# Folding the modulation row behind the first piece of the next unit, and three more units' sums on VectorE

## The chip, the cores and the metric

The kernel runs on one core of a Trainium2 chip. The time is the device time of one execution in microseconds (us), from three runs of the same program. Lower is better.

## The reference, cut to what matters

Two models run one behind the other on the same 256 tokens of width 2048. The first has two layers (`first_block`): a norm, one wide projection `w_in` to 5824 columns, three kinds of attention, a gate and the projection `w_out`. The second has one layer of another kind with a mixture of experts behind it, and its norms are modulated by a row `mod` that depends on nothing but the vector `c`:

```python
def second_block(x, c, ..., ada_w, ada_b, ...):
    c_act = jax.nn.silu(c)                              # 1 x 2048
    mod = (c_act @ ada_w[l] + ada_b[l])[:, None, :]     # 2048 x 12288, a product with one row
    sh1, sc1, g1, sh2, sc2, g2 = jnp.split(mod, 6, axis=-1)
    ...
```

The kernel computes this row while the layers of the first model run, 512 of its 12288 columns at a time, so in 24 parts: 12 in each layer of the first model.

## The kernel before, in words

**Units and pieces.** In each of the two layers (`l` is 0 or 1) TensorE goes through 16 units. Units 0 to 11 are the column blocks of `w_in`, 512 columns each, in the order `ORDER`; unit 2 (`NARROW`) is the narrow one of 192 columns. Units 12 to 15 are `w_out`. A unit is cut into 8 pieces (4 in unit 2) of two 128-row blocks of weights. ScalarE rounds a piece's weights (`w_hi`, L2489), GpSimd computes what the rounding left (L2172), and TensorE multiplies: `by_hi` is eight products with the rounded weights (L2248), `by_lo` four with the remainder (L2259). In `unit` the `by_lo` of a piece comes behind the `by_hi` of the next one. The rounded pieces stand in a ring of four buffers, so ScalarE can be up to four pieces ahead of the last piece that TensorE has finished.

**Steps between the pieces.** Attention for the columns that are already there is cut into steps (transposes, scores, weighted sums), and `unit` is given a list of (piece, step). Before piece `i` it takes the steps placed at `i` or earlier. The order on every engine is written out by hand, and engines run in order: what stands behind a wait waits too.

**The modulation's parts.** Part `p` of layer `l` needs two half loads of `ada_w` (2 MB each), which use ring slots 2 and 3, one behind the other, in the queue of SyncE (`Halves`, L2110). A slot is free when `ada_used` says that the half before it was used up. There are two ways to compute a part. By TensorE: `ada(l, p)` behind the last piece of unit `p` multiplies the 16 blocks of `ada_w` by a column of `c` each (L2298), into four rows of the bank `psTD`; VectorE then adds up the four rows and the bias (`add_row`, L2932 to L2935). By VectorE, for the parts named in `BY_VECTOR`: `mods` does 16 multiply-adds over 128x512 (L2909, L2911), which leave the products summed over the 16 blocks in `ada_sum`, and TensorE only sums over the partitions with one product (L2303), still in `ada` behind the last piece of unit `p`; `add_row` then has one instruction (L2938).

**What stands around part 2 and part 3.** Behind unit 2 come `mla_norm` (transposes) and `mla_up` (products, L2361), and then `ada(l, 2)`. On VectorE the loop turn `p = 2` is: `add_row(2)`, which waits for TensorE's sum; `rotations` (two calls of `rotate`, twelve `TENSOR_TENSOR`, L2775 to L2777); then `mods` of part 3, if it is VectorE's; then the tasks of unit 3, of which there are none. On ScalarE, `store_row(2)` (L2602, and L2597 in `load_b`) waits for the row of `add_row(2)`, and behind it in the same queue come the roundings from piece 3 of unit 3 on. At the top of the turn `p = 3` comes `add_row(3)`.

Of the kernel before, what the change touches and what calls it, by code (L numbers as in the profile page):

```python
# [90 lines left out]
         9: (2, 3, 4, 5, 5, 6, 7), 10: (1, 2, 2, 3, 4, 5, 6, 7, 7, 8), 11: (1, 2, 2, 3, 4, 5, 5, 6, 6, 7, 7, 8),  # L91
         12: (1, 2, 3, 4, 4, 5, 5, 6, 6, 7, 7, 8, 8), 13: (2,)}
MODS = 16
BY_VECTOR = ((0, 2, 4, 5, 6), (2, 4, 5, 6))
MOD_AT = {4: {("mla_rope", 0, 0): 4, ("mla_rope", 0, 1): 9, "end": 16}, 5: {("soft", "M0", 0): 2, ("soft", "M0", 1): 5, ("soft", "M1", 0): 9, "end": 16},
          6: {("out", "M0", 0): 3, ("out", "M0", 1): 8, ("prep_d", 0, 0): 14, "end": 16}}
X_AT = {0: (14, 1), 1: (14, 5), 2: (15, 4), 3: (0, 4)}
# [1777 lines left out]
def program(nc, ctx, a, out):  # L1875
# [4 lines left out]
    def sb(name, shape, dt=f32):  # L1880
        return ctx.enter_context(nc.sbuf_tensor(name, shape, dt))

    def sem(name):
        return ctx.enter_context(nc.semaphore(name))

    def both(name, shape):
# [21 lines left out]
    ada_sum = cb[:, :, :].rearrange("p k n -> p (k n)")  # L1908
# [14 lines left out]
    half = sb("minus_half", [P, 8])  # L1923
# [9 lines left out]
    psS, psO, psTA, psTD = bank[4], bank[5], bank[6], bank[7]  # L1933
# [6 lines left out]
    hu_used, pc_used, ada_used = sem("half_unit_used"), sem("piece_used"), sem("ada_half_used")  # L1940
    x_in, spilled = [sem(f"x_in{n}") for n in range(4)], [sem(f"x_spilled{n}") for n in range(4)]
    x_back, x_hi_ready, sqx_ready, mla_in, in_cst, row_summed = (
        sem(n) for n in ("x_back", "x_rounded", "x_squares", "mla_weights_in", "cst_in", "ada_row_summed"))
# [4 lines left out]
    ta_ready, ta_copied, td_ready, td_copied = (sem(n) for n in ("ta_ready", "ta_copied", "td_ready", "td_copied"))  # L1948
# [120 lines left out]
    def rounded(q):  # L2069

        _, _, _, _, _, ks, width = piece(q)
        return w_hi[:, q % HI_RING, 0:len(ks) * width]
# [16 lines left out]
    def sums(p):  # L2089

        return p + (4 if p > NARROW else 0)
# [109 lines left out]
    def _(pe):  # L2201
# [3 lines left out]
        ta, td = Tally(0, 1), Tally(0, 1)  # L2205
# [5 lines left out]
        def transposes(by_act, sources):  # L2211

            t, ready, cop, ps = (ta, ta_ready, ta_copied, psTA) if by_act else (td, td_ready, td_copied, psTD)
            pe.wait_ge(cop, t.now())
            for i, src in enumerate(sources):
                last = nc.tensor.transpose(ps[:, i * P:(i + 1) * P], src, ident)
            last.then_inc(ready, 1)
            t.next()
# [6 lines left out]
        def x_chunk(l, n):  # L2225

            pe.wait_ge(xo, 1 + 4 * (l - 1) + n + 1) if l else pe.wait_ge(x_in[n], 16)
            for j in (2 * n, 2 * n + 1):
                transposes(j % 2 == 0, [X[:, t, (2 * j + b) * P:(2 * j + b + 1) * P] for b in (0, 1) for t in range(TT)])
                x_done[l, j] = (ta if j % 2 == 0 else td).now()  # L2230
# [5 lines left out]
        def by_hi(q, v, first):  # L2236

            l, u, i, key, _, ks, width = piece(q)
            hi, lo = (x_hi, x_lo) if u < 12 else (y_hi, y_lo)
            if u == 0 or u >= 12:  # L2240
                j = ks[0] // 2
                pe.wait_ge(td_copied if j % 2 else ta_copied, (x_done if u == 0 else y_done)[l, j])
            pe.wait_ge(w_hi_ready, q + 1)
            w = rounded(q).rearrange("p (k n) -> p k n", n=width)
            for part in (hi, lo):
                for n, k in enumerate(ks):
                    for t in range(TT):
                        nc.tensor.matmul(bank[2 * (v % 2) + t][:, 0:width], part(k, t), w[:, n, :],  # L2248
                                         start=first and part is hi and n == 0, stop=False)

        def by_lo(q, v, end):

            l, u, i, key, _, ks, width = piece(q)
            hi = x_hi if u < 12 else y_hi
            pe.wait_ge(w_lo_ready, q + 1)
            w = weights(q, True).rearrange("p (k n) -> p k n", n=width)
            for n, k in enumerate(ks):
                for t in range(TT):
                    last = nc.tensor.matmul(bank[2 * (v % 2) + t][:, 0:width], hi(k, t), w[:, n, :],  # L2259
                                            start=False, stop=end and n == len(ks) - 1)  # L2260
            last.then_inc(pc_used, 1)

        def unit(l, u, steps, bank_free):

            base, n = l * NPC + FIRST[u], PIECES_IN[u]
            queue, behind = list(steps), None
            for i in range(n):
                while queue and queue[0][0] <= i:
                    queue.pop(0)[1]()
                if u < 12:  # L2270
                    v, first, end = sums(u), i == 0, i == n - 1
                    if i == 0:
                        bank_free()
                else:
                    col, rows = OUT_HALVES[2 * (u - 12) + i // 4]
                    v, first, end = 16 + col, rows == 1 and i % 4 == 0, rows == 0 and i % 4 == 3
                    if first:
                        bank_free(col)
                by_hi(base + i, v, first)
                if behind:  # L2280
                    by_lo(*behind)
                behind = (base + i, v, end)
            by_lo(*behind)
            for _, do in queue:
                do()

        def ada(l, p):

            if l + p == 0:
                pe.wait_ge(half_ready, 1)  # L2290
            pe.wait_ge(td_copied, td.now())
            if p not in BY_VECTOR[l]:
                for j in (0, 1):
                    pe.wait_ge(w_in[2 + j], HALVES.loaded["a", l, p, j])
                    w = ring[:, 2 + j, :].rearrange("p (k n) -> p k n", k=8)
                    for k in range(8):
                        g = k % 4
                        last = nc.tensor.matmul(psTD[32 * g:32 * g + 1, :], ccol[:, 8 * j + k:8 * j + k + 1], w[:, k, :],  # L2298
                                                start=j == 0 and k < 4, stop=j == 1 and k >= 4)
                    last.then_inc(ada_used, 1)  # L2300
            else:
                pe.wait_ge(ada_used, 24 * l + 2 * p + 2)
                nc.tensor.matmul(psTD[0:1, :], half[:, 0:1], ada_sum, start=True, stop=True).then_inc(row_summed, 1)  # L2303
            td.next()

        def qk_columns(by_act, group, sources):
# [41 lines left out]
        def mla_norm(l):  # L2348

            pe.wait_ge(cn_ready, l + 1)  # L2350
            cq = lambda b, t: PROJ[:, t, CQ + b * P:CQ + (b + 1) * P]
            for bs in ((0, 1), (2, 3), (4,)):
                transposes(False, [cq(b, t) for b in bs for t in range(TT)])
# [78 lines left out]
        for l in range(LAYERS):  # L2432
            for u in range(12):

                def bank_free():
                    v = sums(u)
                    if v >= 2:
                        pe.wait_ge(pj_copied, 16 * l + v - 1)
                    elif l:
                        pe.wait_ge(xo, 1 + 4 * (l - 1) + 3 + v)  # L2440

                later = steps(l, u)
                if u == 0:
                    later += [((X_AT[3][1] if l else 0), lambda n=n: x_chunk(l, n)) for n in range(4) if n == 3 or not l]
                unit(l, u, later, bank_free)
                if u == NARROW:
                    mla_norm(l)
                    mla_up(l)
                ada(l, u)

            def out_free(col):
                pe.wait_ge(pj_copied, 16 * l + 15 + col) if col < 2 else pe.wait_ge(xo, 1 + 4 * l + col - 1)

            for u in range(12, UNITS):
                later = steps(l, u)
                for n in range(3) if l < LAYERS - 1 else ():
                    if X_AT[n][0] == u:
                        later.append((X_AT[n][1], lambda n=n: x_chunk(l + 1, n)))
                unit(l, u, later, out_free)
# [232 lines left out]
    def _(dve):  # L2692
# [231 lines left out]
        def add_row(l, p):  # L2924
# [3 lines left out]
            if n > 0:  # L2928
                dve.wait_ge(mod_out, 16 * n)
            if p not in BY_VECTOR[l]:  # L2930
                dve.wait_ge(ada_used, 2 * n + 2)
# [4 lines left out]
            else:  # L2936
                dve.wait_ge(row_summed, l * len(BY_VECTOR[0]) + sum(x < p for x in BY_VECTOR[l]) + 1)
                V.scalar_tensor_tensor(ada_row[:, :], psTD[0:1, :], -2.0, ada_b[:, :], ALU.mult, ALU.add).then_inc(td_copied, 1)  # L2938
# [31 lines left out]
        for l in range(LAYERS):  # L2970
# [34 lines left out]
            for p, u in enumerate(ORDER):  # L3005
# [5 lines left out]
                if early:  # L3011
                    task(l, p + 1, *early[0])
                if p and p in BY_VECTOR[l]:
                    mods(l, p, MODS)
# [5 lines left out]
                if p == NARROW:  # L3020
                    rotations(l)
                if p + 1 in BY_VECTOR[l]:
                    mods(l, p + 1, mod_at.table.get("begin", 0) if p + 1 in MOD_AT else MODS)
# [95 lines left out]
```

## Time and profile before

| what | value |
|---|---|
| median of 3 runs | 2451.64 us (2450.39 to 2454.13) |
| the profiled execution | 2450.62 us, span of its trace 2448.8 us |
| TensorE busy | 94% of the span |
| VectorE, ScalarE, GpSimd busy | 37%, 35%, 37% |
| mean granted TensorE clock | 0.983 of full speed |
| first model (both layers) | about 0 to 945 us of the span |

The times of the trace count from the start of the span. A row of a timeline gives the start, the length, the engine, the line of the kernel and the operation, what it writes and reads, how many instructions the row holds, and in brackets how long the engine stood idle before it and what ended that. A granted clock of 1.00 is TensorE's upper level, 2.4 GHz, and 0.50 the lower, 1.2 GHz.

### The profile page before, as it was taken

The page shows a single profiled execution, that of the slowest core. Times are in us where ns is not written, and L with a number is a line of the kernel's source. Part 1 is how long each engine was busy: PE and PEld are TensorE (multiplying, and loading weights), DVE is VectorE, ACT ScalarE, POOL GpSimd, SP SyncE. Part 2 cuts the span into 40 slices and gives each one's busy share as a digit, 9 for nine tenths or more (in the row PEclk, how much of TensorE's full clock was granted, in tenths as well). Part 3 has the DMA queues.
Part 4 walks back from the last instruction along what each step waited for, and adds up shares of the span by engine and source line. Part 5 has one row for each costly group of instructions (what it writes and reads, how often), then busy time and mean ns, then how long its engine had stood idle before and what let it go on. Part 6 is the DMA issues. An engine that isn't in the chain of part 4 may idle for free.

```text
span 2448.8 us, 29997 instructions
## 1 busy us (share of the span) xinstructions
PE 2304.2 (94%) x11863; PEld 1522.7 (62%) x11863; DVE 912.7 (37%) x1495; ACT 852.4 (35%) x1583; POOL 899.5 (37%) x395
## 2 busy tenths in 40 slices
PE   7999999999999998999899898999999999999997
PEld 5677777876777787778787685444444444444442
DVE  5555543125555346155443742122222222222223
ACT  5344454533444443543324742122212221212111
POOL 5566656866666587874333471000000000000000
PEclk9999999999999999999999998999999999999999
DMA  8677665686776661532222329999999999999996
GB/s 325 265 295 287 274 244 238 223 322 251 275 288 253 265 249 62 188 138 87 88 102 99 145 89 393 422 427 428 428 429 428 428 428 428 428 429 428 428 428 269
DMA packets 60805, 716.54 MB, mean 293 GB/s; under 512 B 11024, under 2 KB 11632, under 8 KB 17184
## 3 DMA queue, kind: packets, MB, share of 16 engines
q1 hardware_dynamic: 58800, 712.25, 71.2%
q10 hardware_dynamic: 1904, 2.86, 0.3%
q8 instruction: 73, 1.20, 0.2%
q14 instruction: 28, 0.23, 0.0%
HBM read 710.85 MB, written 4.24 MB: 292 GB/s over the span
## 4 chain that ended last, share of the span: by engine, by line
issue 39%; PE 16%; DVE 3%; ACT 2%; DMA 1%; DVEq 0%; POOLq 0%; POOL 0%; ACTq 0%
PE bank L380 5%; PE bank L434 2%; PE bank L390 2%; PE bank L444 1%; DMA weight_ring<-in_w_in_dram 1%; PE bank L519 1%; PE bank L525 1%; ACT w_hi_parts L2489 1%; PE bank L523 1%; PE bank L623 1%; PE bank L482 0%; PE bank L483 0%; PE bank L480 0%; PE bank L473 0%; PE bank L366 0%
## 5 line engine op out<-in xcount | busy, mean ns | idle before, releaser
L2172 POOL TENSOR_TENSOR weight_ring_parts<-weight_ring,w_hi_parts 128x1024 fp32r<-128x1024 f32 (+2 forms) x368 | 871.9, 2390 | 554.8 <-ACT w_hi_parts L2489 553.3
L2489 ACT ACTIVATE w_hi_parts<-weight_ring 128x1024 fp32r<-128x1024 f32 (+2 forms) x368 | 376.7, 1042 | 435.9 <-PE bank L2259 175.5
L1509 POOL TENSOR_TENSOR rms_out<-rms_in,minus_half 128x2 f32<-128x2 f32 x2 | 1.4, 698 | 963.6 <-DVE rms_in L1855 950.4
L1592 PE MATMUL bank<-weight_ring,qk_t 128*64 128x512 f32 x1024 | 229.2, 603 | 17.8 <-DMA weight_ring<-in_expert_w_up_dram 17.8
L2248 PE MATMUL bank<-w_hi_parts,h_t_parts 128*128 128x512 f32 (+1 forms) x768 | 213.3, 401 | 2.0 <-ACT w_hi_parts L2489 2.0
L2248 PE MATMUL bank<-w_hi_parts,x_res_parts 128*128 128x512 f32 (+1 forms) x768 | 198.5, 382 | 0.0
L2259 PE MATMUL bank<-weight_ring_parts,h_t_parts 128*128 128x512 f32 (+1 forms) x768 | 193.3, 380 | 0.0
L1592 PEld LDWEIGHTS bank<-weight_ring,qk_t 128*64 128x64 f32 x1024 | 77.4, 139 | 166.6 <-issue 166.6
L2248 PEld LDWEIGHTS bank<-w_hi_parts,h_t_parts 128*128 128x128 f32 x768 | 133.0, 190 | 47.1 <-issue 17.4
L2248 PEld LDWEIGHTS bank<-w_hi_parts,x_res_parts 128*128 128x128 f32 x768 | 140.5, 189 | 29.6
L2259 PEld LDWEIGHTS bank<-weight_ring_parts,h_t_parts 128*128 128x128 f32 x768 | 139.8, 188 | 28.4
L1833 DVE TENSOR_TENSOR dist<-dist_masked,bank 128x512 f32<-128x512 f32 x16 | 11.0, 688 | 351.0 <-PE bank L1592 351.0
L1818 DVE SCALAR_TENSOR_TENSOR qk_t<-bank,slot_gate,proj 128x512 f32<-128x512 f32 x64 | 48.1, 751 | 240.9 <-PE bank L1623 240.9
L1689 ACT ACTIVATE p_t<-bank 128x512 f32<-128x512 f32 x16 | 9.6, 597 | 344.3 <-PE bank L1605 344.3
L1541 PE MATMUL bank<-p_buf,y 128*128 128x128 f32 x1024 | 123.3, 280 | 4.2 <-ACT qk_t L1668 3.1
L1592 PE MATMUL bank<-w_hi,qk_t 128*64 128x512 f32 x256 | 114.3, 600 | 12.0 <-DMA h_t<-in_expert_w_up_dram 12.0
L1541 PEld LDWEIGHTS bank<-p_buf,y 128*128 128x128 f32 x1024 | 119.0, 195 | 7.1 <-ACT qk_t L1668 5.9
L1592 PE MATMUL bank<-h_t,qk_t 128*64 128x512 f32 x256 | 114.5, 601 | 0.0
L1623 PE MATMUL bank<-weight_ring,p_t 128*64 128x512 f32 x512 | 113.0, 594 | 0.8 <-ACT p_t L1689 0.8
L1592 PE MATMUL bank<-proj,qk_t 128*64 128x512 f32 x512 | 112.8, 593 | 0.0
L380 PE MATMUL bank<-w_hi_parts,h_t_parts 128*128 128x512 f32 (+1 forms) x352 | 97.8, 400 | 7.3 <-ACT w_hi_parts L2489 5.7
L1668 ACT ACTIVATE qk_t<-bank,conv_w_t 128x128 f32<-128x128 f32 x256 | 94.5, 456 | 19.5 <-PE bank L1541 19.5
(473 smaller groups left out, 3581.1 us busy)
## 6 DMA issues: line engine op xcount, KB each, us to landing
weight_ring<-in_w_in_dram SPq DMA_DIRECT2D x64, 2048.0 KB, 7.6
weight_ring<-in_ada_w_dram SPq DMA_DIRECT2D x48, 2048.0 KB, 12.5
weight_ring<-in_expert_w_gate_dram SPq DMA_DIRECT2D x32, 2048.0 KB, 26.9
weight_ring<-in_expert_w_up_dram SPq DMA_DIRECT2D x32, 2048.0 KB, 18.3
weight_ring<-in_expert_w_down_dram SPq DMA_DIRECT2D x32, 2048.0 KB, 24.1
weight_ring<-in_w_out_dram SPq DMA_DIRECT2D x24, 2048.0 KB, 8.7
proj<-in_expert_w_gate_dram SPq DMA_DIRECT2D x16, 2048.0 KB, 26.8
proj<-in_expert_w_up_dram SPq DMA_DIRECT2D x16, 2048.0 KB, 15.4
```

What stands on the lines that cost most here:

```text
L380: mm(bank[2 * (v % 2) + t][:, 0:width], part[:, k, t * P:(t + 1) * P], w[:, n, :], start=first and part is hi and n == 0, stop=False)
L390: last = mm(bank[2 * (v % 2) + t][:, 0:width], hi[:, k, t * P:(t + 1) * P], w[:, n, :], start=False, stop=end and n == len(ks) - 1)
L434: mm(bank[2 * (p % 2) + t][:, :], y_at(part, kb, t), w[:, n, :], start=r == FIRST2[c] and part == "hi" and n == 0, stop=False)
L1541: last = mm(ps[:, i * P:(i + 1) * P], H[:, t, k * P:(k + 1) * P], m.gm[:, t, :], start=t == 0, stop=t == TT - 1)
L1592: last = mm(bank[side][s, :], m.xg[:, 8 * j + k, s], weights(hu + e, 8)[:, k, :], start=j == 0 and k == 0, stop=j == 1 and k == 7)
L1623: last = mm(bank[4 + n % 2][s, :], m.hidt[:, f, s], weights(hu + e, 4)[:, f, c * U:(c + 1) * U], start=f == 0, stop=f == 3)
L1668: last = A_(m.xg[:, k, :], bank[2 + (tx.n - 1) % 2][:, i * P:(i + 1) * P], ACT.Identity, scale=m.gsc2[:, k:k + 1], bias=m.shc2[:, k:k + 1])
L1818: V.scalar_tensor_tensor(m.ye[:, c], bank[4 + n % 2][:, :], m.slot_gate[:, :], m.g2[:, c], ALU.mult, ALU.mult).then_inc(m.dn_copied, 1)
L2172: nc.gpsimd.tensor_tensor(weights(split, True), weights(split, False), rounded(split).bitcast(f32), ALU.subtract)\
L2248: nc.tensor.matmul(bank[2 * (v % 2) + t][:, 0:width], part(k, t), w[:, n, :], start=first and part is hi and n == 0, stop=False)
L2259: last = nc.tensor.matmul(bank[2 * (v % 2) + t][:, 0:width], hi(k, t), w[:, n, :], start=False, stop=end and n == len(ks) - 1)
L2489: A_(rounded(split), weights(split, False), ACT.Copy).then_inc(w_hi_ready, 1)
```

## The change

Parts 1 and 3 of layer 1 and part 3 of layer 0 move from TensorE to VectorE (`BY_VECTOR`). For the parts 0 to 5 that are VectorE's, the product that sums over the partitions moves from the end of unit `p` to the place before piece 1 of unit `p + 1`, so behind `by_hi` of piece 0 (`FOLD_AT`, `fold`); it stands ahead of other steps with the same place. Part 6 stays behind its unit. Nothing else is changed: `mods` and `add_row` keep their places in VectorE's order.

```diff
-BY_VECTOR = ((0, 2, 4, 5, 6), (2, 4, 5, 6))
+BY_VECTOR = ((0, 2, 3, 4, 5, 6), (1, 2, 3, 4, 5, 6))
+FOLD_AT = {0: 1, 1: 1, 2: 1, 3: 1, 4: 1, 5: 1}
...
-            pe.wait_ge(td_copied, td.now())
             if p not in BY_VECTOR[l]:
+                pe.wait_ge(td_copied, td.now())
...
                     last.then_inc(ada_used, 1)
-            else:
-                pe.wait_ge(ada_used, 24 * l + 2 * p + 2)
-                nc.tensor.matmul(psTD[0:1, :], half[:, 0:1], ada_sum, start=True, stop=True).then_inc(row_summed, 1)
+                td.next()
+            elif p not in FOLD_AT:
+                fold(l, p)
+
+        def fold(l, p):
+
+            pe.wait_ge(td_copied, td.now())
+            pe.wait_ge(ada_used, 24 * l + 2 * p + 2)
+            nc.tensor.matmul(psTD[0:1, :], half[:, 0:1], ada_sum, start=True, stop=True).then_inc(row_summed, 1)
             td.next()
...
+                if u - 1 in BY_VECTOR[l] and u - 1 in FOLD_AT:
+                    later = sorted([(FOLD_AT[u - 1], lambda: fold(l, u - 1))] + later, key=lambda x: x[0])
                 unit(l, u, later, bank_free)
```

## Rows read from the trace of the kernel before

**Rows 1.** The page's first part: busy time of each engine, share, instructions.

```profile
PE 2304.2 (94%) x11863; PEld 1522.7 (62%) x11863; DVE 912.7 (37%) x1495; ACT 852.4 (35%) x1583; POOL 899.5 (37%) x395
```

**Rows 2.** Timeline of TensorE, layer 0, from the end of `mla_up` into unit 4.

```profile
107.37 1.02 PE L2303 MATMUL bank<-ada_sums,minus_half 128*1 128x512 f32 x2
108.32 1.19 PE L2248 MATMUL bank<-w_hi_parts,h_t_parts 128*128 128x512 f32 x4
...
130.31 3.62 PE L2298 MATMUL bank<-weight_ring,c_col 128*1 128x512 f32 x32
133.85 1.20 PE L2248 MATMUL bank<-w_hi_parts,h_t_parts 128*128 128x512 f32 x4
...
135.80 0.60 PE L2216 MATMUL bank<-cst,proj 128*128 128x128 f32 x4
```

**Rows 3.** Timeline of VectorE, layer 0: sums of part 2, its row, the rotations.

```profile
90.81 0.75 DVE L2909 TENSOR_SCALAR bank<-weight_ring,c_col 128x512 f32<-128x512 f32 x1
...
102.67 0.75 DVE L2911 SCALAR_TENSOR_TENSOR ada_sums<-weight_ring,c_col,bank 128x512 f32<-128x512 f32 x1
108.53 0.68 DVE L2938 SCALAR_TENSOR_TENSOR ada_part<-bank,ada_part 1x512 f32<-1x512 f32 x1 [5.12 <-PE bank L2303]
109.37 0.42 DVE L2775 TENSOR_TENSOR rope_q<-proj,cos_t 128x256 f32<-128x256 f32 x1 [0.16 <-DVE ada_part L2938]
...
111.88 2.38 DVE L2775 TENSOR_TENSOR rope_k<-proj,cos_t 128x128 f32<-128x128 f32 x1
...
119.71 0.29 DVE L2777 TENSOR_TENSOR rope_k<-rope_k,rope_tmp 128x128 f32<-128x128 f32 x1
```

**Rows 4.** Timeline of ScalarE, its queue and GpSimd in the same stretch of layer 0.

```profile
109.30 0.23 ACTq L2602 DMA_DIRECT2D mod_scratch<-ada_part  x1
...
110.52 1.06 ACT L2489 ACTIVATE w_hi_parts<-weight_ring 128x1024 fp32r<-128x1024 f32 x1 [1.95 <-issue]
...
111.66 2.45 POOL L2172 TENSOR_TENSOR weight_ring_parts<-weight_ring,w_hi_parts 128x1024 fp32r<-128x1024 f32 x1 [10.83 <-ACT w_hi_parts L2489]
...
113.25 1.06 ACT L2489 ACTIVATE w_hi_parts<-weight_ring 128x1024 fp32r<-128x1024 f32 x1 [1.67 <-PE bank L2259]
...
114.39 2.40 POOL L2172 TENSOR_TENSOR weight_ring_parts<-weight_ring,w_hi_parts 128x1024 fp32r<-128x1024 f32 x1 [0.28 <-ACT w_hi_parts L2489]
...
121.35 1.06 ACT L2489 ACTIVATE w_hi_parts<-weight_ring 128x1024 fp32r<-128x1024 f32 x1 [1.66 <-PE bank L2259]
```

**Rows 5.** Timeline of VectorE and GpSimd in layer 0 from 277 us.

```profile
277.73 9.83 POOL L2172 TENSOR_TENSOR weight_ring_parts<-weight_ring,w_hi_parts 128x1024 fp32r<-128x1024 f32 x4
...
278.64 1.52 DVE L2850 SCALAR_TENSOR_TENSOR row_rec<-row_rec,lam,row_sum 128x2 f32<-128x2 f32 x1
...
280.20 5.11 DVE L2852 SCALAR_TENSOR_TENSOR p_buf<-p_buf,row_rec 128x256 f32<-128x256 f32 x2
```

**Rows 6.** TensorE after an idle stretch, and windows (busy times, then clock, DMA).

```profile
951.03 4.53 PE L366 MATMUL bank<-p_t,proj 128*128 128x128 f32 x24 [6.08 <-DVE p_t L1047]
...
951.03:956.03 5.00, 4.66 (x25) 4.49 (x26) 1.99 (x4) 0.76 (x2) 4.92 (x3) 0.66 0.00 0
1095.68:1101.68 6.00, 6.00 (x31) 6.00 (x32) 1.32 (x2) 0.42 (x1) 4.22 (x2) 0.54 0.01 3
```

**Rows 7.** Timelines of layer 1: TensorE around units 3 and 4, and VectorE's last rotation.

```profile
567.45 1.02 PE L2303 MATMUL bank<-ada_sums,minus_half 128*1 128x512 f32 x2
...
590.40 3.61 PE L2298 MATMUL bank<-weight_ring,c_col 128*1 128x512 f32 x32
...
595.89 0.60 PE L2216 MATMUL bank<-cst,proj 128*128 128x128 f32 x4
...
579.80 0.29 DVE L2777 TENSOR_TENSOR rope_k<-rope_k,rope_tmp 128x128 f32<-128x128 f32 x1
```

**Rows 8.** Loads of `ada_w`: issues of two halves, a wait for one, layer 1's unit 1.

```profile
132.27 2.04 SPq L2110 DMA_DIRECT2D weight_ring<-in_ada_w_dram  x2
...
142.84 0.75 DVE L2909 TENSOR_SCALAR bank<-weight_ring,c_col 128x512 f32<-128x512 f32 x1 [2.52 <-DMA weight_ring<-in_ada_w_dram]
...
508.81 2.04 SPq L2110 DMA_DIRECT2D weight_ring<-in_ada_w_dram  x2
...
532.37 3.61 PE L2298 MATMUL bank<-weight_ring,c_col 128*1 128x512 f32 x32
```

## The prediction, made before the changed kernel was run

> **What bounds the kernel now.** I read the page's busy shares first, then the timeline of TensorE around each `ada`, then those of the engines that feed it. TensorE is busy for 94% of the span, the others for some 37% [rows 1]. In the two layers its timeline has almost no bracket: from one unit into the next it goes without a stop, so whatever is taken off its list is gained, if nothing new comes late. A part by TensorE holds it from 130.31 to 133.85, 3.54 us; a part by VectorE only from 107.37 to 108.32, 0.95 us [rows 2]. So the question is not what the 32 removed instructions cost, but whether VectorE has the sum ready when TensorE gets to it. For that the reader has to look at what VectorE does ahead of the sums: in turn 2 it waits for TensorE's product (5.12 us in the bracket), then rotates from 109.37 to 120.00, and would begin the sums of part 3 only then [rows 3].
>
> **Part 1 of layer 1.** It takes away 3.54 and adds 0.95: 2.6 us gained, if the sum is ready. The halves are issued from 508.81 on; elsewhere VectorE got the first half 10.6 us after the issue (132.27 to 142.84) [rows 8], so here at 519.4. The sixteen sums of part 2 took from 90.81 to 103.42, 12.6 us [rows 3]; here they end at about 532.0. TensorE ends unit 1 at 532.37 [rows 8] and asks behind piece 0, about 2 us later. Ready, by some 2 us. The slots come free earlier than before, so the loads behind it are not later. VectorE's row sum is one instruction rather than four, and the norm behind it waits for ScalarE's squares, as it does now. Gain 2.6 us.
>
> **Moving the product of part 2, layer 0.** The product leaves the front of unit 3 and comes behind piece 0's eight products, which take 1.95 us (133.85 to 135.80) [rows 2]. TensorE's own list is as long as before. But everything that waits for the product is 1.95 us later: `add_row(2)` begins at 110.48, the rotations at 111.3. ScalarE is caught as well: `store_row(2)` waits for that row, and the rounding of piece 3 stands behind it (110.52, right behind the store at 109.30), and GpSimd's remainder for it starts at 111.66 [rows 4]. Now that becomes 113.6. Before, GpSimd was kept to TensorE's pace from there: the next rounding waited for TensorE (113.25) and left a gap of 0.28 us on GpSimd [rows 4]. TensorE's own pace for pieces 1 and on is unchanged, so the roundings of pieces 4 to 7 keep nearly their times (the last begins at 121.35 [rows 4]), while GpSimd is 2 us behind. Its five instructions then run back to back, from 113.6 on.
>
> This matters to the rotations, which read two operands from SBUF each. In the trace such an instruction takes 0.42 us undisturbed, and 2.38 us where GpSimd is at work (111.88) [rows 3]. Where GpSimd has gaps, a second rotation slips through between two of its instructions; three of the twelve are held up and the end is 120.00. Where it has none, each such instruction of VectorE costs a whole one of GpSimd: against four GpSimd instructions in 9.83 us, one took 1.52 and the next two 5.11 together [rows 5]. So the rotations 7 to 11 cost 2.46 us each (9.83 / 4): five GpSimd instructions from 113.6 end at 125.9, the last rotation at 126.2. That is 6.2 us later than now: 1.95 by the place, 4.25 by the loss of the gaps.
>
> The Trainium skill (SBUF — State Buffer, "Who interferes with whom") says that an instruction of VectorE with two SBUF inputs and one of GpSimd that reads SBUF lock each other out for a whole instruction, and that "Issue order, not op shape, decides who blocks". The rows agree on the size, and it is the rule that speaks against this change. Taken literally, VectorE might get in first and hold up GpSimd, by a few tenths each time; the rotations would then end at about 122 and the time would be that of the first rival below. The sums of `mods` read one operand from SBUF and one from a bank, which by the same section is free of the lock.
>
> **Part 3, layer 0.** The sums start at 126.2, take 12.6 us, and end at 138.8. They can't start earlier: they stand behind the rotations in VectorE's order, and all their data has long been there. TensorE, without the product ahead of unit 3 and with it inside, ends the unit at 130.31 as before, does piece 0 of unit 4 until 132.26, and waits there, with the whole rest of unit 4 behind the wait. The product starts at 138.9 and ends at 139.85. At this same point of its list it is at 135.80 now [rows 2]. So this part, which was to give 2.6 us, costs 4.05, and TensorE stands idle for 6.65 us.
>
> **The clock after such a stop.** After 6.08 us of idle time TensorE had a granted clock of 0.66 over the next 5 us, so 3.4 us of it at the lower level (1.2 GHz), a loss of 1.7 us. After another stop it had 0.54 over 6 us, a loss of 2.8 us [rows 6]. I take 1.7, the stop that is nearest in length; the bounds are 0 and 2.8.
>
> **Parts 2 and 3, layer 1.** The same chain, 2.6 us earlier on TensorE. Unit 3 starts at 567.45 - 2.6 = 564.85, the product at 566.8, so 0.65 us before its present time. The rotations end at 580.1 now [rows 7]; I take 580.1 - 0.65 + 4.25 = 583.7, the sums end at 596.3, the product at 597.35, against 595.89 for the same point now [rows 7]: 1.45 us lost with the 2.6 us of part 1 already counted. The clock takes another 1.7.
>
> **Parts 0, 4 and 5** are moved only. Their products are 0.95 us wherever they stand, and VectorE gets 1.95 us more for them; their rows come 1.95 us later, ahead of tasks that wait for steps at piece 1 or 2 of the unit anyway. In unit 4 the sums of part 4 wait for their load until 142.84 [rows 8], about as long as the new stop lasts. Nothing, between -0.5 and +0.5 us in all.
>
> **The sum.** Layer 0: 4.05 + 1.7 = +5.75. Layer 1: 1.45 + 1.7 = +3.15. Together +8.9 on the profiled execution's 2450.62: 2459.5. The median of the runs is 1.02 above that execution, so I forecast 2460.5 us.
>
> **The rivals.**
>
> *The rotations keep their length.* VectorE's instructions find gaps, or get in first. Then only the 1.95 us count: the sums of part 3 end at 134.6 in layer 0, and TensorE passes the point at 135.65 for 135.80 now; in layer 1 at 593.1 for 595.89. That is -0.2 and -2.8, with stops of 2.3 us, and between 0 and 1.7 us of clock each: -3.0 to +0.4, a median of 2448.7 to 2452.1, say 2450.4. For it: two of the twelve slipped through a gap in the trace of before. Against it: they did so only where GpSimd had a gap.
>
> *The sums are hidden, and the change does what it says on paper* (the rival on the other side, faster). Three parts give 2.6 us each, 7.8 in all: 2443.8. The mechanism is that the sums of part 3 overlap with the rotations' place or end by 132.26; it decides at 2.4 us less on VectorE than even the first rival needs. Nothing in the rows offers that.
>
> *More stops than these.* If the loads of part 1 in layer 1 land over 2.3 us later than the row that I used says, the product waits in unit 2 too and the norm behind it slides, 1 to 4 us; or each stop costs 2.8 us of clock and a sixth rotation is held up: up to 8.9 + 2 x 1.1 + 2 x 2.5 = +16, 2468.
>
> *That the change doesn't do what it says* can be left out: the moved product and the three parts are in the lists of all engines.
>
> **How the numbers follow.** The forecast (rotations held up for the whole of GpSimd's stretch, one or two of them more or less, clock 0 to 2.8) 0.60; rotations as now 0.26; hidden 0.05; more stops 0.09. The forecast's own range is +5.5 (no clock) less one slipped rotation in a layer (2.5), to +11.1: 2454.6 to 2462.7. For 8 in 10 the range takes in most of the first rival above and the beginning of the last: 2451 to 2465. A measurement of this kernel can tell about 0.2%, 4.9 us, from no change. Over 2456.5 lies most of the forecast and all of the last rival: 0.62. Within lies the rest of the forecast and nearly all of the first rival: 0.33. Faster by over 0.2%: 0.05.
>
> **What would show each step.** In the trace after: a bracket of 6 to 7 us ahead of L2303's product in unit 4 of both layers, released by VectorE's sums; seven or eight of the twelve rotations undisturbed and five at about 2.5 us, with GpSimd's five instructions without a gap between them; a clock below 1.00 in the 5 us behind each bracket; no bracket at the product in unit 2 of layer 1, and TensorE 2.6 us earlier there against layer 0's delay. Brackets of 2 us would mean the first rival, none the second. The forecast is wrong if GpSimd's gaps stay, because then the largest term, 4.25 us in each layer, is gone.

## The result, and the profile after

The changed kernel takes 2459.09 us (median of 7 runs, 2457.05 to 2465.87), against 2451.64 for the kernel before, measured beside it (median of 7 runs, 2447.38 to 2454.13). The ratio is 1.004, with a 95% interval of 1.0027 to 1.0052; it is estimated from all runs of both kernels and isn't the quotient of the two medians, which is 1.003. The changed kernel is slower by 0.4%. The forecast was 2460.5, in a range of 2451 to 2465. The profiled execution of the changed kernel took 2459.09 us with a span of 2457.3 us.

The page's busy shares hardly moved, as in [rows 1]; what changed is when the engines work:

```profile
PE 2301.7 (94%) x11773; PEld 1522.5 (62%) x11773; DVE 952.9 (39%) x1534; ACT 851.8 (35%) x1583; POOL 897.8 (37%) x395
```

TensorE's timeline in layer 0, units 2 to 4, to be read against [rows 2] (columns: start, duration, engine, line, operation; the bracket is idle time before the row and what ended it):

```profile
106.73 1.50 PE L2249 MATMUL bank<-w_hi_parts,h_t_parts 128*128 128x512 f32 x4
...
109.08 1.02 PE L2310 MATMUL bank<-ada_sums,minus_half 128*1 128x512 f32 x2
...
130.20 1.16 PE L2249 MATMUL bank<-w_hi_parts,h_t_parts 128*128 128x512 f32 x4
...
138.47 1.87 PE L2310 MATMUL bank<-ada_sums,minus_half 128*1 128x512 f32 x2 [6.21 <-DVE ada_sums L2920]
140.27 1.11 PE L2217 MATMUL bank<-cst,proj 128*128 128x128 f32 x4
```

Unit 3 begins at 106.73 without its product, which now comes behind piece 0, at 109.08. Unit 3 ends, and unit 4 begins, at 130.20; before, unit 3 ended at 130.31 and part 3's 32 products came next. Then the bracket that was not there before: TensorE stands for 6.21 us and is released by VectorE's last sum of part 3. The transposes that follow are at 140.27, where they were at 135.80 [rows 2].

VectorE, ScalarE and GpSimd in the same stretch, against [rows 3, 4]:

```profile
110.24 0.68 DVE L2947 SCALAR_TENSOR_TENSOR ada_part<-bank,ada_part 1x512 f32<-1x512 f32 x1 [6.95 <-PE bank L2310]
111.07 0.43 DVE L2784 TENSOR_TENSOR rope_q<-proj,cos_t 128x256 f32<-128x256 f32 x1 [0.16 <-DVE ada_part L2947]
...
111.58 1.06 ACT L2498 ACTIVATE w_hi_parts<-weight_ring 128x1024 fp32r<-128x1024 f32 x1 [3.16 <-DVEq L2949]
...
112.72 12.40 POOL L2173 TENSOR_TENSOR weight_ring_parts<-weight_ring,w_hi_parts 128x1024 fp32r<-128x1024 f32 x5 [11.64 <-ACT w_hi_parts L2498]
...
113.12 2.51 DVE L2786 TENSOR_TENSOR rope_q<-rope_q,rope_tmp 128x256 f32<-128x256 f32 x1
115.67 2.37 DVE L2784 TENSOR_TENSOR rope_k<-proj,cos_t 128x128 f32<-128x128 f32 x1
117.96 2.49 DVE L2785 TENSOR_TENSOR rope_tmp<-proj,sin_t 128x128 f32<-128x128 f32 x1
120.48 2.38 DVE L2786 TENSOR_TENSOR rope_k<-rope_k,rope_tmp 128x128 f32<-128x128 f32 x1
122.89 2.37 DVE L2784 TENSOR_TENSOR rope_k<-proj,sin_t 128x128 f32<-128x128 f32 x1
125.19 0.28 DVE L2785 TENSOR_TENSOR rope_tmp<-proj,cos_t 128x128 f32<-128x128 f32 x1
...
126.49 11.05 DVE L2920 SCALAR_TENSOR_TENSOR bank<-weight_ring,c_col,bank 128x512 f32<-128x512 f32 x14
137.58 0.75 DVE L2920 SCALAR_TENSOR_TENSOR ada_sums<-weight_ring,c_col,bank 128x512 f32<-128x512 f32 x1
```

The row of part 2 is added at 110.24 (before: 108.53), and ScalarE's rounding of piece 3, which waits for it, starts at 111.58 (before: 110.52). GpSimd's five remainders are one group of 12.40 us with no gap, and exactly five rotations take 2.4 to 2.5 us each, one for each of GpSimd's instructions. The rotations last from 111.07 to 125.79, 14.7 us, for 10.6 before (109.37 to 120.00). The sums behind them end at 138.3.

Layer 1, TensorE, against [rows 7]:

```profile
551.26 0.66 PE L2217 MATMUL bank<-cst,proj 128*128 128x128 f32 x4 [0.97 <-DVE qk_t L2749]
...
553.95 7.98 PE L2368 MATMUL bank<-y,qk_t 128*128 128x512 f32 x24 [0.62 <-issue]
...
593.06 1.16 PE L2249 MATMUL bank<-w_hi_parts,h_t_parts 128*128 128x512 f32 x4 [1.31 <-ACT w_hi_parts L2498]
...
600.03 1.87 PE L2310 MATMUL bank<-ada_sums,minus_half 128*1 128x512 f32 x2 [4.89 <-DVE ada_sums L2920]
601.83 1.12 PE L2217 MATMUL bank<-cst,proj 128*128 128x128 f32 x4
...
607.04 0.60 PE L2217 MATMUL bank<-cst,proj 128*128 128x128 f32 x4
```

The same stop, 4.89 us, and one of 1.31 us ahead of it that was in no step of the prediction: TensorE waits for the rounded weights of unit 4. The first row serves to follow part 1: the same transposes start at 548.29 in the kernel before.

**Where the time went.** I compare the two traces at points that both have. From the end of unit 0 of layer 0 (49.44 before, 49.18 after) to the end of unit 0 of layer 1 (506.85, 512.43) it is 457.41 and 463.25: **+5.84 us for layer 0**. From there to the wait that ends the first model, [rows 6] at 951.03 and in the changed kernel

```profile
957.38 2.93 PE L367 MATMUL bank<-p_t,proj 128*128 128x128 f32 x12 [6.07 <-DVE p_t L1048]
```

it is 444.18 and 444.95: **+0.77 us for layer 1**. I call this point the end of the first model. The code behind it is the same in both kernels and took 1497.8 and 1499.9 us in these two executions. In the ten profiled executions of this study it took between 1497.8 and 1501.9, so single executions scatter there by more than most terms of the sum, and below I set the times of this point beside the medians.

### The profile page after: what moved, and what is told of

It reads as the page before. It is cut to its first block, busy times and chain, and to the rows that moved or that the text cites. A ratio compares the mean times of both kernels' runs of the same rounds, so it can differ in the third digit from the quotient of the medians.

```text
span 2457.3 us, 29863 instructions
## 1 busy us (share of the span) xinstructions
PE 2301.7 (94%) x11773; PEld 1522.5 (62%) x11773; DVE 952.9 (39%) x1534; ACT 851.8 (35%) x1583; POOL 897.8 (37%) x395
## 4 chain that ended last, share of the span: by engine, by line
issue 39%; PE 17%; DVE 3%; ACT 2%; DMA 1%; DVEq 0%; POOLq 0%; POOL 0%; ACTq 0%
PE bank L381 5%; PE bank L391 2%; PE bank L435 2%; PE bank L445 1%; PE bank L520 1%; DMA weight_ring<-in_w_in_dram 1%; PE bank L526 1%; PE bank L524 1%; ACT w_hi_parts L2498 1%; PE bank L624 1%; PE bank L483 0%; PE bank L484 0%; PE bank L481 0%; PE bank L474 0%; PE bank L367 0%
## 5 line engine op out<-in xcount | busy, mean ns | idle before, releaser
L2920 DVE SCALAR_TENSOR_TENSOR bank<-weight_ring,c_col,bank 128x512 f32<-128x512 f32 x168 | 126.8, 755 | 5.4
```

The source lines that it names most:

```text
L2920: ins = V.scalar_tensor_tensor(acc if k < MODS - 1 else ada_sum, w, ccol[:, k:k + 1], acc, ALU.mult, ALU.add)
```

## The experiments

All eight are the changed kernel with one thing altered, and each was timed in rounds with the kernel before. The ratio is to that kernel, with its 95% interval; the last column is the start of the product that marks the end of the first model in the profiled execution. The ratio isn't the quotient of a row's median and the 2451.64: the runs of the kernel before that each experiment was timed beside had medians of 2452.98 (sums alone, part 2's product back, sums first, rounding ahead) and 2452.21 (the other four).

| kernel | median us | ratio (95%) | end of first model |
|---|---|---|---|
| before | 2451.64 | | 951.03 |
| after | 2459.09 | 1.0040 (1.0027 to 1.0052) | 957.38 |
| sums alone | 2450.53 | 0.9997 (0.9987 to 1.0006) | 948.88 |
| place alone | 2453.47 | 0.9997 (0.9987 to 1.0008) | 949.98 |
| part 1 alone | 2448.24 | 0.9986 (0.9976 to 0.9996) | 947.92 |
| part 2's product back | 2444.94 | 0.9971 (0.9960 to 0.9982) | 942.37 |
| sums first | 2446.62 | 0.9978 (0.9968 to 0.9987) | 943.14 |
| rounding ahead | 2451.86 | 0.9994 (0.9985 to 1.0003) | 953.30 |
| no remainder | 2443.34 | 0.9964 (0.9949 to 0.9978) | 941.73 |
| part 1 too | 2444.67 | 0.9970 (0.9958 to 0.9981) | 943.01 |

The theory on trial is that of the prediction: the later place of part 2's product takes the gaps from GpSimd, the rotations are then held up for all of its stretch, and the sums of part 3 behind them are late. The rivals are that the sums are late by themselves, that the later place alone is enough, and that VectorE's load as such is the cause.

### The sums alone, with all products in their old places

```diff
-FOLD_AT = {0: 1, 1: 1, 2: 1, 3: 1, 4: 1, 5: 1}
+FOLD_AT = {}
```

> The three parts move to VectorE, and every product over the partitions stays at the end of its unit. My theory (the moved product of part 2 makes the sums of part 3 late: 1.95 us by its place, some 4 us because GpSimd then runs without gaps and holds up the rotations): the rotations end at 120.0 in layer 0 as before the change, the sums of part 3 at 132.6, TensorE asks for them at 130.3, so it stands for 2.4 us at the end of unit 3 in each layer, not for 5 to 6 us; part 1 gives 2.6 us; in all -3.0 us against before, plus 0 to 1.7 us of lower clock for each stop: 2448 to 2452. Rival A (VectorE's list is simply too long for part 3, wherever the product of part 2 stands): the stop is at least as long as with the change, 6 us, since TensorE asks 2 us sooner, and the time is 2459 or more.

Measured: 2450.53 us, as expected, and no difference from before that the interval shows. Its TensorE waits for the sums of part 3 in both layers:

```profile
132.34 1.02 PE L2310 MATMUL bank<-ada_sums,minus_half 128*1 128x512 f32 x2 [2.30 <-DVE ada_sums L2920]
...
590.85 1.36 PE L2310 MATMUL bank<-ada_sums,minus_half 128*1 128x512 f32 x2 [2.30 <-DVE ada_sums L2920]
```

The rotations last from 109.04 to 119.66, 10.6 us as in [rows 3]. For part 3 the move therefore saves 2.6 us and gives back 2.30. In layer 0 the stop of the changed kernel is 2.7 times as long, so the sums by themselves are not its cause.

### Part 2's product back in front of unit 3, all else as in the change

```diff
-FOLD_AT = {0: 1, 1: 1, 2: 1, 3: 1, 4: 1, 5: 1}
+FOLD_AT = {0: 1, 1: 1, 3: 1, 4: 1, 5: 1}
```

> The whole change, but the product of part 2 stays at the end of its unit; those of parts 0, 1, 3, 4 and 5 are moved. My theory: rotations as before the change (three of twelve held up, end at 120.0 in layer 0), sums of part 3 end at 132.6, TensorE asks at 132.3 and stands for 0.5 us; each part gives its 2.6 us less that: -6.8 us against before, 2445, and no stretch at the lower clock in unit 4. Rival A (VectorE's list is too long for part 3 anyway): stops of 5 us or more in unit 4, 2457 or more. Rival B (a moved product costs something by itself, by breaking up the pieces or by keeping ScalarE's stores late): about 2450, with no stop.

Measured: 2444.94 us, as expected, and faster than both kernels. VectorE, GpSimd and TensorE in layer 0, then TensorE in layer 1:

```profile
112.17 2.37 DVE L2784 TENSOR_TENSOR rope_k<-proj,cos_t 128x128 f32<-128x128 f32 x1
114.46 0.28 DVE L2785 TENSOR_TENSOR rope_tmp<-proj,sin_t 128x128 f32<-128x128 f32 x1
114.69 2.40 POOL L2173 TENSOR_TENSOR weight_ring_parts<-weight_ring,w_hi_parts 128x1024 fp32r<-128x1024 f32 x1 [0.30 <-ACT w_hi_parts L2498]
114.77 2.47 DVE L2786 TENSOR_TENSOR rope_k<-rope_k,rope_tmp 128x128 f32<-128x128 f32 x1
117.28 0.29 DVE L2784 TENSOR_TENSOR rope_k<-proj,sin_t 128x128 f32<-128x128 f32 x1
...
132.98 1.02 PE L2310 MATMUL bank<-ada_sums,minus_half 128*1 128x512 f32 x2 [0.32 <-DVE ada_sums L2920]
...
585.41 1.16 PE L2249 MATMUL bank<-w_hi_parts,h_t_parts 128*128 128x512 f32 x4 [0.94 <-ACT w_hi_parts L2498]
...
587.41 1.02 PE L2310 MATMUL bank<-ada_sums,minus_half 128*1 128x512 f32 x2
```

A held-up rotation and a quick one alternate: GpSimd has its gaps again (0.22 to 0.30 us) and the rotations take 10.6 us. The stop of 2.30 is down to 0.32, because part 3's own product still stands behind piece 0 (2.30 - 1.95 = 0.35). In layer 1 there is no stop at the product; the 0.94 us ahead of it is a wait for unit 4's weights, which is taken up below. This one number in a table is worth 957.38 - 942.37 = 15.0 us at the end of the first model. Two stops of 6.21 and 4.89 us, less the 0.32, and the lower clock behind them (1.6 and 2.8, below) make 15.2.

### The new places alone, with the sums of before

```diff
-BY_VECTOR = ((0, 2, 3, 4, 5, 6), (1, 2, 3, 4, 5, 6))
+BY_VECTOR = ((0, 2, 4, 5, 6), (2, 4, 5, 6))
```

> The products of parts 0, 2, 4 and 5 (and of none besides) are moved behind the first piece of the next unit, and parts 1 and 3 stay with TensorE as before the change. My theory: the rotations are held up as with the change and end at about 126 in layer 0, but nothing waits for them before unit 4: TensorE has no stop, the time is that of before, within 1 us; at most a few tenths are gained where VectorE was late by 0.6 us at part 6. Rival B (moving the products costs by itself): 1 to 2 us slower for each moved product, 2455 or more.

Measured: 2453.47 us, as expected no difference from before. VectorE's first and last held-up rotations and GpSimd's group:

```profile
113.66 12.39 POOL L2173 TENSOR_TENSOR weight_ring_parts<-weight_ring,w_hi_parts 128x1024 fp32r<-128x1024 f32 x5 [12.06 <-ACT w_hi_parts L2498]
114.06 2.52 DVE L2786 TENSOR_TENSOR rope_q<-rope_q,rope_tmp 128x256 f32<-128x256 f32 x1
...
123.84 2.37 DVE L2784 TENSOR_TENSOR rope_k<-proj,sin_t 128x128 f32<-128x128 f32 x1
```

The place alone brings GpSimd's closed group and the five held-up rotations, 14.7 us in all, and here it costs nothing, because no sums of part 3 stand behind them. So neither half of the change is slow. The stop needs both.

### The sums of part 3 ahead of the rotations on VectorE

```diff
-                if p == NARROW:
-                    rotations(l)
                 if p + 1 in BY_VECTOR[l]:
                     mods(l, p + 1, mod_at.table.get("begin", 0) if p + 1 in MOD_AT else MODS)
+                if p == NARROW:
+                    rotations(l)
```

> The whole change, and on VectorE the sums of part 3 come ahead of the rotations. My theory: the sums run from 111.3 to 124 in layer 0, free of GpSimd, the rotations behind them end at about 130, TensorE finds the sums ready in unit 4: no stop in either layer, -7.8 us against before, 2444. Rival C (the rotations are then what comes late: they run into GpSimd's next stretch from 130 on at 2.5 us each, and the copies of unit 4 stand behind them): a stop of 2 to 6 us in unit 4 ahead of the transposes, 2446 to 2456.

Measured: 2446.62 us, faster than before, but 2.6 us above the 2444 that I expected. At the end of the first model the 7.8 us are there (951.03 less 943.14 is 7.9); the medians show only some 5.4 of them (a ratio of 0.9978). In the two profiled executions the unchanged code behind that point took 1500.1 us and, in the kernel before, 1497.8, the least of the ten; why the rest is lost stays open. VectorE and GpSimd in layer 0, then TensorE's product of part 3 in layer 0 and in layer 1:

```profile
112.13 11.05 DVE L2920 SCALAR_TENSOR_TENSOR bank<-weight_ring,c_col,bank 128x512 f32<-128x512 f32 x14
112.99 9.49 POOL L2173 TENSOR_TENSOR weight_ring_parts<-weight_ring,w_hi_parts 128x1024 fp32r<-128x1024 f32 x4 [10.65 <-ACT w_hi_parts L2498]
...
123.99 1.33 DVE L2784 TENSOR_TENSOR rope_q<-proj,cos_t 128x256 f32<-128x256 f32 x1
...
128.79 0.29 DVE L2786 TENSOR_TENSOR rope_k<-rope_k,rope_tmp 128x128 f32<-128x128 f32 x1
...
132.32 1.02 PE L2310 MATMUL bank<-ada_sums,minus_half 128*1 128x512 f32 x2
...
587.53 1.02 PE L2310 MATMUL bank<-ada_sums,minus_half 128*1 128x512 f32 x2
```

Both brackets are gone. The sums run beside GpSimd at 0.79 us each (11.05 / 14), as they do without it, and GpSimd keeps 2.37 us per instruction (9.49 / 4). The rotations behind it find GpSimd nearly done and take 5.1 us. VectorE does the same work in both orders, so its load as such is not the cause; the order is. That the sums aren't disturbed agrees with the Trainium skill (SBUF — State Buffer, "Who interferes with whom"), by which a VectorE instruction with at most one SBUF input, outside the modes that use two ports, doesn't contend with GpSimd. Each sum reads one 128x512 operand from SBUF, a column of `c` beside it, and the running sum from a bank.

### ScalarE's rounding ahead of the store of part 2's row

```diff
-                split_to(q + sum_place(p) + AHEAD)
+                split_to(q + sum_place(p) + AHEAD + (1 if p == NARROW else 0))
                 store_row(l, p)
```

> The whole change, and ScalarE rounds piece 3 of unit 3 before it waits for the row of part 2, not behind it, so that GpSimd gets it some 3 us earlier and is kept to TensorE's pace from there, with its gaps. My theory: the gaps let a second rotation through, the rotations end at about 122.4 in layer 0 and not at 125.8, the stop in unit 4 is 3 us and not 6.2, in both layers: 6 to 7 us less than with the change, some 2452 with the lower clock still paid. Rival D (the hold-up has nothing to do with the gaps; each rotation that meets GpSimd waits for a whole instruction): the rotations end within 1 us of 125.8 and the time stays at 2459.

Measured: 2451.86 us, as expected. GpSimd gets the first rounded piece before the row is stored. Its rows in layer 0, and TensorE's stops:

```profile
115.95 2.46 POOL L2173 TENSOR_TENSOR weight_ring_parts<-weight_ring,w_hi_parts 128x1024 fp32r<-128x1024 f32 x1 [2.46 <-ACT w_hi_parts L2498]
118.61 2.53 POOL L2173 TENSOR_TENSOR weight_ring_parts<-weight_ring,w_hi_parts 128x1024 fp32r<-128x1024 f32 x1 [0.20 <-ACT w_hi_parts L2498]
121.33 2.42 POOL L2173 TENSOR_TENSOR weight_ring_parts<-weight_ring,w_hi_parts 128x1024 fp32r<-128x1024 f32 x1 [0.19 <-ACT w_hi_parts L2498]
...
136.58 1.02 PE L2310 MATMUL bank<-ada_sums,minus_half 128*1 128x512 f32 x2 [2.75 <-DVE ada_sums L2920]
...
597.18 1.02 PE L2310 MATMUL bank<-ada_sums,minus_half 128*1 128x512 f32 x2 [2.80 <-DVE ada_sums L2920]
```

With gaps of 0.2 us back between GpSimd's instructions the rotations take 11.2 us (112.73 to 123.91) rather than 14.7. The product of part 2 is as late as in the change, and yet the stop falls from 6.21 to 2.75. That separates the two terms of the prediction: some 3.5 us are the lost gaps. The 2.75 that are left are the 0.32 us that stay even with part 2's product back, the 1.95 of the place and the 0.5 or so by which these rotations are longer than 10.6, together 2.8.

### GpSimd's remainders of unit 3 nearly left out

```diff
-                nc.gpsimd.tensor_tensor(weights(split, True), weights(split, False), ...
+                n = 8 if left_out(split) else weights(split, True).shape[-1]
+                nc.gpsimd.tensor_tensor(weights(split, True)[:, 0:n], weights(split, False)[:, 0:n], ...
```

> The whole change, but for the pieces 3 to 7 of unit 3, in both layers, GpSimd's remainder is computed over 8 columns only, and TensorE takes the rounded weights a second time in its place. That leaves out part of the projection of unit 3, so it measures the hold-up of the rotations alone and is no version of the kernel. My theory (GpSimd's instructions hold them up): all twelve rotations at 0.42 or 0.29 us, done within some 5 us of the row of part 2 in place of 14.9, the sums of part 3 ready at about 128.5 in layer 0, ahead of TensorE, no stop and no lower clock in unit 4 of either layer; first model 14 us shorter than with the change, 2444. Rival E (they are slow for another reason, such as the loads or ScalarE's writes): five of them still take 2.4 us each and the stop stays at 6.

Two things aren't in these lines: `left_out` picks the pieces 3 to 7 of unit 3, and for them TensorE reads the rounded weights a second time in the remainder's place. The projection of unit 3 is then incomplete, so this is a measuring kernel and no version to use.

Measured: 2443.34 us. VectorE's last rotation and TensorE's product, layer 0 (lines are six further down here):

```profile
114.64 0.29 DVE L2792 TENSOR_TENSOR rope_k<-rope_k,rope_tmp 128x128 f32<-128x128 f32 x1
...
131.81 1.02 PE L2316 MATMUL bank<-ada_sums,minus_half 128*1 128x512 f32 x2
```

All twelve rotations take 0.28 to 0.42 us, together 4.2 us (110.75 to 114.93), and there is no stop, with the products and the sums exactly where the change puts them. So GpSimd is what makes the rotations long: 10.5 us of their 14.7.

### Part 1 of layer 1 alone

```diff
-BY_VECTOR = ((0, 2, 3, 4, 5, 6), (1, 2, 3, 4, 5, 6))
+BY_VECTOR = ((0, 2, 4, 5, 6), (1, 2, 4, 5, 6))
```

> As with the change, but part 3 stays with TensorE in both layers; only part 1 of layer 1 moves to VectorE, and the products are moved. My theory: no stop in unit 4, 2.6 us gained in layer 1, so -2.6 us against before, 2449 to 2450, and the end of the first model 2.6 us earlier in the trace. Rival F (part 1's sums wait for their load, and TensorE for them in unit 2): a stop in unit 2 of layer 1, and nothing gained.

Measured: 2448.24 us, ratio 0.9986 (0.9976 to 0.9996), with no bracket at the product of part 1: 3.1 us less at the end of the first model in one profiled execution of each, where 2.6 were expected. This part of the change does what it says.

### Part 1 of layer 0 given to VectorE too, on top of the sums first

```diff
-BY_VECTOR = ((0, 2, 3, 4, 5, 6), (1, 2, 3, 4, 5, 6))
+BY_VECTOR = ((0, 1, 2, 3, 4, 5, 6), (1, 2, 3, 4, 5, 6))
```

> The change with the sums of part 3 ahead of the rotations, and part 1 of layer 0 given to VectorE as well. My theory (each part by VectorE is worth 2.6 us as long as its sum is ready when TensorE asks): the two halves are issued at 51, the first lands 12 us later, the sums end near 75.8 and TensorE asks at about 75.5: a stop of 0 to 1 us in unit 2 of layer 0, and about 10 us less than before, 2442 to 2443. Rival F (the load is what decides): a stop of 3 us or more there, with a stretch at the lower clock in the short unit 2, and the time of the same order without this part, 2446 or more.

Measured: 2444.67 us, where 2442 to 2443 was expected. Its ratio, 0.9970, lies inside the interval of the kernel it starts from (0.9968 to 0.9987), so the medians don't show whether the 2.6 us arrived. At the end of the first model they didn't: 943.01 against 943.14. TensorE in layer 0:

```profile
75.30 1.02 PE L2310 MATMUL bank<-ada_sums,minus_half 128*1 128x512 f32 x2 [0.16 <-DVE ada_sums L2920]
...
131.51 1.16 PE L2249 MATMUL bank<-w_hi_parts,h_t_parts 128*128 128x512 f32 x4 [1.23 <-ACT w_hi_parts L2498]
```

And the windows over `mla_up` in this kernel and, below it, in the sums-first kernel (length, then busy time and count of TensorE, its weight loads, VectorE, ScalarE and GpSimd, then clock, DMA share, GB/s):

```profile
86.84:100.40 13.56, 11.97 (x31) 6.51 (x32) 11.62 (x17) 4.65 (x7) 7.00 (x3) 0.75 0.64 241
```

```profile
89.46:100.70 11.24, 9.35 (x31) 5.38 (x32) 9.62 (x15) 4.54 (x7) 5.35 (x3) 1.00 0.80 314
```

The sum is ready in time (0.16 us of wait), and ahead of `mla_up` this kernel leads the sums-first one by 2.62 us (86.84 against 89.46), 0.54 of which it had before the part's place (at 49.94 and 50.48). Then the clock takes the lead away: this kernel is granted 0.75 over the stretch and needs 13.39 us to its end (100.23), the other 1.00 and 11.07 us (100.53). What is left is 0.30. At unit 4 there is a wait of 1.23 us for weights that the sums-first kernel doesn't have there (its unit 4 starts at 130.37, without a bracket), and this kernel is 1.14 us behind. In layer 1 the clock falls the other way, 7.98 us for the 24 products of `mla_up` against 9.68, and the two end level. So the part gives 2.1 us where its own products stood, and the clock and a load took them again in this execution. Both differ between the traces of kernels that have the same work there, so what the part is worth in the median is not shown.

## Why the prediction was right, and where its terms were not

**What held.** In layer 0 every link came out within 1 us of where it was put: GpSimd's five back to back from 112.72 (113.6 was said), rotations end at 125.8 (126.2), sums end at 138.3 (138.8), TensorE reaches its wait at 132.3, the stop is 6.21 us (6.65). Layer 0 cost +5.84 in the accounting above, +5.75 in the sum; but the terms as measured (6.21 of stop and 1.6 of clock, less the 2.6 us of part 3) make 5.2, and the other 0.6 lies in tenths elsewhere in the layer, so the sum fits better than its terms. The two terms of the late rotations also stand one by one: the closed group of GpSimd appears with the place alone, goes when the rounding is put ahead, and takes 3.5 us of the stop with it. The whole term, rotations of 14.7 us for 10.6, is 4.1 (4.25 was said). The literal reading of the Trainium skill's rule, by which VectorE might get in first and hold up GpSimd by a few tenths, fell as the prediction's own reading had it: GpSimd lost 0.1 us per instruction (12.40 / 5 = 2.48 against 9.49 / 4 = 2.37), VectorE 2.1. The rule's size, a whole instruction, agrees.

**Part 1 of layer 1** was said to be ready by 2 us and to give 2.6. The sums end at 537.61 and TensorE's product starts at 539.72, a margin of 2.1. The delay against before shrinks across it from 5.58 us (508.81 to 514.39) to 2.97 (548.29 to 551.26): 2.61 us.

**The sum of layer 1 was mis-sized:** +3.15 said, +0.77 measured. The clock was put too small, the wait for unit 4's weights and two gains were missing, and together they leave 2.4 us that the forecast had too many:

- The clock behind the stop: 1.7 said. From the product to the second transposes the trace of after has 138.47 to 144.26 in layer 0 and 600.03 to 607.04 in layer 1. The same instructions take 4.20 us in the kernel with part 2's product back (132.98 to 137.18). So the lower clock cost 1.6 us in layer 0, and 2.8 in layer 1, the upper bound that I had. The windows of after say the same:

```profile
138.47:143.47 5.00, 5.00 (x15) 2.89 (x16) 0.68 (x1) 0.60 (x1) 0.98 (x1) 0.66 1.00 426
600.03:605.03 5.00, 5.00 (x12) 2.81 (x13) 0.68 (x1) 0.60 (x1) 2.29 (x1) 0.50 1.02 429
551.26:563.60 12.34, 10.75 (x35) 6.16 (x36) 10.68 (x16) 5.31 (x9) 6.98 (x3) 1.00 0.59 219
```

- Unit 4's weights. I had put nothing for what the 3.54 us of part 3's 32 products covered. In layer 1 TensorE is at unit 4 before its weights are rounded and waits 1.31 us. The stop for the sums is shorter by as much (4.89, not 6.21), so here it cost little of its own. This was the step "Parts 2 and 3, layer 1", which takes TensorE into unit 4 without a stop and asks only for the sums. Whether the wait comes depends on the load: without those products it is there when ScalarE gets the weights more than 7.8 us after the load's issue, and as long as the excess. In the changed kernel that was 7.76 us in layer 0 (121.23 to 128.99), with no wait, and 9.15 in layer 1 (582.71 to 591.86), with 1.31. With part 2's product back it was 8.76 in layer 1, with 0.94 of wait, and with part 1 too 9.06 in layer 0, with 1.23. The sums-first kernel, at 7.62 and 7.48, has no such wait in either layer.
- A gain that no step had: over `mla_up` in layer 1 the clock is 1.00 (last row above) and 24 products take 7.98 us; in the trace of before the same 24 take 9.68 us. That is 1.7 us, with the same three short waits ahead of it in both. Whether it belongs to the change or to this execution is not shown: over the same products the ten traces spread from 7.98 to 11.02 us.
- Later in layer 1 the delay shrinks from 7.84 us (end of unit 4, 618.62 to 626.46) to 6.35 at the end of the first model, 1.5 us that no step had. Two waits of TensorE for VectorE that the trace of before has there are gone:

```profile
634.64 2.39 PE L2324 MATMUL bank<-qk_t 128*128 128x256 f32 x8 [0.46 <-DVE p_buf L2831]
...
679.30 1.02 PE L2303 MATMUL bank<-ada_sums,minus_half 128*1 128x512 f32 x2 [0.64 <-DVE ada_sums L2911]
```

  They answer for 1.1 us of it. A wait of 0.45 us for ScalarE at 692.42 is new, and two later waits for VectorE are 0.65 us shorter together (1.40 and 1.51 for 1.65 and 1.91), so the waits give 1.3 of the 1.5. I take it that VectorE gains on TensorE there because TensorE is the later one; that was not tried.

**The median.** The profiled executions stand 6.35 us apart at the end of the first model and 2.1 more behind it, in code that is the same; that is scatter of single executions. So +8.9 came out as 8.5 between the profiled executions and as 7.45 between the medians. The total came nearer than its parts deserve: the 2.4 us too many in layer 1 were made up by 2.1 us that no term had.

**The first rival** ("the rotations keep their length") named 2.3 us for the stop and 2450.4 us. That is the kernel with the rounding ahead, 2.75 us and 2451.86: its mechanism was sound, and only GpSimd's missing gaps kept it from being the case. One link was mis-sized: the row's lateness was to delay ScalarE's rounding and GpSimd behind it by the whole 1.95 us. The row came 1.71 us later (110.24 for 108.53), the rounding 1.06 (111.58 for 110.52, released by VectorE's queue), and GpSimd 1.06 (112.72 for 111.66). It was enough to close the gaps.

**A version that beats both** kernels comes out of this: put the product of part 2 back in front of unit 3, or put part 3's sums ahead of the rotations. They give 0.9971 (0.9960 to 0.9982) and 0.9978 (0.9968 to 0.9987); their intervals overlap, so which is the better stays open.

## What to carry to other kernels

When work is moved to an idle engine, look at what stands ahead of it in that engine's order and at whose pace that runs. Here twelve small instructions took 4.2, 5.1, 10.6, 11.2 or 14.7 us, depending on how much another engine worked beside them and with what gaps. Two halves of a change that each cost nothing cost 7.5 us together, and the change without its one harmful move is 14 us faster than with it (2444.94 for 2459.09), so test the halves apart and together. And before work is taken off the bounding engine, list everything that its time was covering, loads of weights included.

## What the runs showed of the hardware that I had not expected

- **Same waits, different clock.** Ahead of `mla_up` TensorE has the same three waits (0.97, 0.97 and 0.62 us) in all traces, yet the granted clock over the stretch is 1.00, 0.86 or 0.75, and the 24 products take 7.98 us (changed kernel, layer 1), 9.68 (before, layer 1), 10.62 (with part 1 too, layer 0) or 11.02 (sums alone, layer 1). I found nothing in the rows that tells which it will be.
- **A short stop can be as dear as a long one.** From the product of part 3 to the first transposes the kernel with the sums alone takes 2.90 us in layer 0 (132.34 to 135.24) and 4.47 in layer 1 (590.85 to 595.32), behind the same stop of 2.30 us: one shows no lower clock, the other loses 1.6 us. With the rounding ahead both stops (2.75 and 2.80) lose 1.6 (5.79 us to the second transposes for 4.20), and after the 4.89 of the changed kernel, which a wait of 1.31 us and one piece of work preceded, it was 2.8.
- **One load, many durations.** From the issue of the load of unit 4's first weights to the moment when ScalarE starts on them it took 7.5 us in both layers of the kernel before (121.34 to 128.83, 581.43 to 588.93), and 9.1 in layer 1 of the changed one (582.71 to 591.86). Over the ten traces and both layers it is between 7.47 and 9.15. What it shares the queues with there was not tried, and stays open.
